# Output projection of a hybrid encoder: seven products of block halves in place of eight

## The reference, cut to what matters

```python
y_a = (on + bonus) * silu(g_a)      # RWKV heads, normalised per head, 384 columns
y_b = o * silu(g_b)                 # attention heads, 384 columns
y_c = u * sv * silu(g_c)            # spatial gating, 256 columns
y = concatenate([y_a, y_b, y_c], axis=-1) @ w_out      # (tokens, 1024) @ (1024, 1024)
return x + gate[:, None, :] * y
```

## Time and profile before

| What | us |
|---|---|
| median of 3 runs (4828.7 to 4844.89) | 4836.14 |
| profiled execution, its own time | 4841.52 |
| span of the profile | 4839.7 |
| TensorE busy in the span | 4595.1 (95%) |
| VectorE busy | 3230.5 (67%) |
| GpSimd busy | 972.8 (20%) |
| first to last matmul of L2407, layer 0 | 2115.2 to 2442.9 |
| the same, layer 1 | 4523.4 to 4834.4 |

### The profile page before, as it was taken

One profiled execution on the slowest core, in us unless ns is written; L12 is line 12 of the kernel. 1 busy time (PEld: TensorE's weight loads), 2 busy tenths in 40 slices (PEclk: granted clock), 3 DMA queues, 4 the chain that ended last, 5 costly groups with the idle time before them and its releaser, 6 DMA issues. The chain is left out here.

```text
span 4839.7 us, 121929 instructions
## 1 busy us (share of the span) xinstructions
PE 4595.1 (95%) x51708; PEld 2830.3 (58%) x51708; DVE 3230.5 (67%) x4926; ACT 1969.3 (41%) x4238; POOL 972.8 (20%) x1638
## 2 busy tenths in 40 slices
PE   7999999989997999989989999999899989999899
PEld 6788444457775445444468884444577754444454
DVE  4555378746656989966545554787466669999665
ACT  1121455535555555521111214655355655555211
POOL 3444000013332000011134440000133310000111
PEclk9999999999999999999999999999999999999999
DMA  6232556556554121155342325565566641211443
GB/s 229 95 125 88 210 175 233 181 144 165 160 160 107 30 46 33 51 176 207 126 157 96 122 76 211 186 225 182 156 164 164 170 94 29 46 40 45 166 166 115
DMA packets 577852, 647.70 MB, mean 134 GB/s; under 512 B 233936, under 2 KB 458896, under 8 KB 567712
## 3 DMA queue, kind: packets, MB, share of 16 engines
q1 hardware_dynamic: 576720, 638.81, 42.3%
q10 hardware_dynamic: 592, 1.10, 0.1%
HBM read 372.64 MB, written 267.13 MB: 132 GB/s over the span
## 5 line engine op out<-in xcount | busy, mean ns | idle before, releaser
L2083 ACT ACTIVATE att_pr<-ps,att_nb 128x512 f32<-128x512 f32 (+1 forms) x960 | 588.0, 628 | 367.1 <-DVE att_nb L2112 367.1
L2407 PE MATMUL ps<-w_out,fin_yT 128*128 128x512 f32 x1280 | 568.5, 597 | 1.3 <-ACT fin_yT L2269 1.3
L2107 DVE TENSOR_REDUCE att_mx<-ps 128x2 f32<-128x1024 f32 (+1 forms) x408 | 492.2, 1206 | 10.1 <-PE ps L2005 10.1
L2129 DVE STREAM_TRANSPOSE att_PT<-att_pr 128x1024 f32<-128x1024 f32 x384 | 473.0, 1232 | 1.0 <-ACT att_pr L2083 1.0
L2039 PE MATMUL ps<-att_PT,att_V 128*32 128x256 f32 x6144 | 408.3, 381 | 10.9 <-issue 7.7
L2407 PEld LDWEIGHTS ps<-w_out,fin_yT 128*128 128x128 f32 x1280 | 238.8, 191 | 273.4 <-issue 273.4
L2005 PE MATMUL ps<-qk 96*32 96x512 f32 (+1 forms) x3840 | 393.7, 530 | 1.5 <-ACT att_pr L2083 1.5
L625 PE MATMUL ps<-feat_Ts,feat_Ss 128*128 128x256 f32 x1680 | 374.8, 379 | 0.6 <-DVE feat_Ts L529 0.6
L1023 PE MATMUL ps<-w_both,prep_hT 128*128 128x512 f32 (+1 forms) x832 | 354.1, 581 | 0.0
L625 PEld LDWEIGHTS ps<-feat_Ts,feat_Ss 128*128 128x128 f32 x1680 | 319.5, 190 | 44.8 <-issue 1.4
L2065 POOL TENSOR_TENSOR att_mm<-att_mx,att_fold 128x8 f32<-128x8 f32 (+1 forms) x408 | 83.2, 204 | 1061.0 <-DVE att_mx L2107 1061.0
(11 more groups left out here) (300 smaller groups left out, 8673.1 us busy)
## 6 DMA issues: line engine op xcount, KB each, us to landing
s_sc<-prep_sc SPq DMA_DIRECT2D x20, 3072.0 KB, 8.9
scan_src<-s_sc SPq DMA_DIRECT2D x104, 384.0 KB, 5.1
s_qkt<-qT SPq DMA_DIRECT2D x40, 576.0 KB, 4.1
s_zf<-feat_co SPq DMA_DIRECT2D x88, 256.0 KB, 2.4
src<-s_sc SPq DMA_DIRECT2D x56, 384.0 KB, 4.9
s_ht<-feat_hT SPq DMA_DIRECT2D x10, 2048.0 KB, 17.2
s_zt<-st SPq DMA_DIRECT2D x80, 256.0 KB, 3.7
fin_z<-s_zt SPq DMA_DIRECT2D x30, 576.0 KB, 5.4
```

The lines of the kernel that those rows point to most:

```text
L2083: last = a.activation(pr[:, m % 4, w * i:w * (i + 1)], ps[:, b0 + w * i // G, w * i % G:w * i % G + w], ACT.Exp, bias=nb[:, m % 2, i:i + 1 ...
L2107: v.tensor_reduce(mx[:, m % 2, 0:n], ps[:, b0:b0 + 2, :].rearrange("p b (u k) -> p (b u) k", u=n // 2), AX.X, ALU.max).then_inc(maxed, 1)
L2129: v.transpose(into, pr[:, m % 4, :].rearrange("p (u k q) -> p u k q", u=n, q=SUB)).then_inc(flipped, 1)
L2407: last = pe.matmul(b, yT[n % TPG][:, k, :], wo[:, k, G * c:G * (c + 1)], start=(k == 0), stop=(k == KD - 1))
```

## The change: what it does

Tiles are taken in pairs p = 0 to 9. Pair 0 is multiplied as before (four `direct` halves). For pairs 1 to 9 the 256 x 1024 by 1024 x 1024 product is split into 2 x 2 blocks (A by token tile and by half of the features, B by halves of rows and columns), and seven block products P1 to P7 of 4 matmuls each replace eight:

- GpSimd makes the sums of weights once per layer (`sum_weights`, 8 instructions of 128x1024), four sums of tokens per pair (`sum_tokens`, 128x512: S1 to S4), and all four additions to the residual x (`add`, 128x512).
- ScalarE copies P1 to SBUF (`keep_first`). VectorE makes U2 = P1 + P6 and U3 = U2 + P7 (`partial`), and the blocks C11 (one instruction), C22, C21 and C12 (an addition and a multiplication by the gate each) in `block_of`.
- P1 and P2 share PSUM bank 0, P6 and P7 bank 1, P5 and P3 bank 2, P4 has bank 3. The units sv, ya, yb, yc share banks 4 and 5, by `Uses(2, BANK_U)`.
- TensorE's order for a pair is P1, P6, sv(a), P2, the turns of a, [modulation], P7, P5, sv(b), P4, the turns of b, P3, with a and b the two tiles of the next pair.
- The loads of x are taken out of the other loads of a tile and come after its store; the modulation weights have two buffers for eight; the modulation rows are turned at the stage's end.

The core of the diff (indentation shortened):

```diff
-order = []
-for n in range(NT):
-    if n == 0:
-        order += [("sv", 0), ("yc", 0), ("ya", 0), ("yb", 0)]
-    order += [("p", n, 0)]
-    if n + 1 < NT:
-        order += [("sv", n + 1), ("ya", n + 1), ("yb", n + 1), ("yc", n + 1)]
-    order += [("p", n, 1)]
-uses = Uses(BANK_M)
+PAIRS, HK = NT // 2, KD // 2
...
+BANK_X, BANK_Y, BANK_V, BANK_Z, BANK_U = 0, 1, 2, 3, 4
+DIRECT = ((0, 1), (1, 1), (0, 0), (1, 0))
+SEVEN = ("P1", "P6", "P2", "P7", "P5", "P4", "P3")
+order = [("sv", 0), ("yc", 0), ("ya", 0), ("yb", 0), ("sv", 1), ("ya", 1), ("yb", 1), ("yc", 1)]
+for n in range(2, NT):
+    order += [("sv", n), ("ya", n), ("yb", n), ("yc", n)]
+uses = Uses(2, BANK_U)
 for u in order:
     uses.add(u, "act" if u[0] in ("yb", "yc") else "dve")
...
+    B11, B12, B21, B22 = (wo[:, HK * i:HK * (i + 1), G * j:G * (j + 1)] for i in range(2) for j in range(2))
+    N1, N2, N4, N3 = wsum[:, 0], wsum[:, 1], wsum[:, 2], B12
+    S1, S2, S3, S4 = (sums[:, j] for j in range(4))
...
+            for p in range(PAIRS + 1):
+                if more and p < KD:
+                    if p >= 2:
+                        sp.wait_ge(ada_used, p - 1)
+                    sp.dma_start(ada[:, p % 2, :], d["ada_w"][:, (l + 1) * KD + p, 0:2 * D]).then_inc(ada_in[p], 16)
+                for n in (2 * p, 2 * p + 1):
+                    if n + TPG < NT:
+                        wait_turned(sp, n)
+                        load_own(n + TPG)
+                        load_heads(n + TPG)
+                if p % 2 and 2 * p + 2 < NT:
+                    wait_for(sp, ("ya", 2 * p + 1))
+                    load_gates((2 * p + 2) // TPG)
+                if p:
+                    for n in (2 * p - 1, 2 * p - 2):
+                        if p == 1:
+                            sp.wait_ge(added0, len(DIRECT))
+                        else:
+                            sp.wait_ge(added, added_at(p - 1, "C21" if n % 2 else "C12"))
+                        store(n)
+                    for n in (2 * p - 1, 2 * p - 2):
+                        if n + TPG < NT:
+                            sp.wait_ge(sent[n % TPG], 16 * here(n)[1])
+                            load_x(n + TPG)
...
+            def keep_first(p):
...
+            for n in range(NT + 2):
+                if n < NT:
+                    open_gates(n)
+                    squares(n)
+                if n % 2 == 0 and n >= 4:
+                    keep_first(n // 2 - 1)
+                if n < NT:
+                    for name in ("yb", "yc") if n else ("yc", "yb"):
+                        turned_out((name, n))
...
+            def sum_weights(n, half):
+                to, one, two = ((N1, B12, B11), (N2, B22, N1), (N4, B21, N2), (N3, B22, B12))[n]
+                k = slice(HK // 2 * half, HK // 2 * (half + 1))
+                if n in (1, 2):
+                    g.wait_ge(w_summed, 2 * n)
+                if n == 3:
+                    g.wait_ge(w_summed, 2)
+                    g.wait_ge(done, done_at(0, (1, 1)))
+                g.tensor_tensor(to[:, k, :], one[:, k, :], two[:, k, :], ALU.subtract).then_inc(w_summed, 1)
+            def sum_tokens(p, n):
+                one, two = yT[2 * p % TPG], yT[(2 * p + 1) % TPG]
+                A11, A12, A21, A22 = one[:, 0:HK, :], one[:, HK:KD, :], two[:, 0:HK, :], two[:, HK:KD, :]
+                to, a_, b_, op = ((S1, A21, A22, ALU.add), (S2, S1, A11, ALU.subtract), (S3, A11, A21, ALU.subtract), (S4, A12, S2, ALU.subtract))[n]
+                if n == 0:
+                    wait_turned(g, 2 * p)
+                    wait_turned(g, 2 * p + 1)
+                if n in (1, 3):
+                    g.wait_ge(y_summed, summed_at(p, n))
+                if p > 1:
+                    g.wait_ge(done, done_at(p - 1, ("P5", "P6", "P7", "P3")[n]))
+                g.tensor_tensor(to, a_, b_, op).then_inc(y_summed, 1)
+            def add(p, what):
+                t, j, c = {"C11": (t11, 0, 0), "C12": (t12, 0, 1), "C21": (t21, 1, 0), "C22": (t22, 1, 1)}[what]
+                n, w = 2 * p + j, slice(G * c, G * (c + 1))
+                wait_x(g, n)
+                if what == "C11":
+                    g.wait_ge(evicted, evicted_at(p, what))
+                else:
+                    g.wait_ge(gated, 3 * (p - 1) + ("C22", "C21", "C12").index(what) + 1)
+                g.tensor_tensor(x[n % TPG][:, w], x[n % TPG][:, w], t[:, :], ALU.add).then_inc(added, 1)
+            root_v(0)
+            root_a(0)
+            root_v(1)
+            sum_weights(0, 0)
+            root_a(1)
+            sum_weights(0, 1)
+            root_v(2)
+            sum_weights(1, 0)
+            sum_weights(1, 1)
+            root_a(2)
+            sum_weights(2, 0)
+            sum_weights(2, 1)
+            root_v(3)
+            sum_weights(3, 0)
+            root_a(3)
+            sum_weights(3, 1)
+            for p in range(1, PAIRS):
+                more_tiles = p + 1 < PAIRS
+                sum_tokens(p, 0)
+                sum_tokens(p, 1)
+                if more_tiles:
+                    root_v(2 * p + 2)
+                sum_tokens(p, 2)
+                if p > 1:
+                    add(p - 1, "C21")
+                    add(p - 1, "C12")
+                if more_tiles:
+                    root_a(2 * p + 2)
+                sum_tokens(p, 3)
+                add(p, "C11")
+                if more_tiles:
+                    root_v(2 * p + 3)
+                add(p, "C22")
+                if more_tiles:
+                    root_a(2 * p + 3)
+            add(PAIRS - 1, "C21")
+            add(PAIRS - 1, "C12")
...
+            def residual(i):
...
+            def partial(p, what):
+                v.wait_ge(done, done_at(p, "P6" if what == "U2" else "P7"))
+                v.wait_ge(kept, p)
+                if p > 1:
+                    v.wait_ge(evicted, evicted_at(p - 1, "C12" if what == "U2" else "C21"))
+                v.tensor_tensor((u2 if what == "U2" else u3)[:, :], s1[:, :], ps[:, BANK_Y, :], ALU.add).then_inc(evicted, 1)
+            def block_of(p, what):
+                t, bank, after = {"C11": (t11, BANK_X, "P2"), "C22": (t22, BANK_V, "P5"), "C21": (t21, BANK_Z, "P4"), "C12": (t12, BANK_V, "P3")}[what]
+                v.wait_ge(done, done_at(p, after))
+                if p > 1:
+                    v.wait_ge(added, added_at(p - 1, what))
+                else:
+                    v.wait_ge(added0, len(DIRECT))
+                if what == "C11":
+                    v.tensor_tensor(t[:, :], ps[:, bank, :], gate[:, min(p // 2, 1), 0:G], ALU.mult).then_inc(evicted, 1)
+                    return
+                v.wait_ge(evicted, evicted_at(p, "U2" if what == "C12" else "U3"))
+                v.tensor_tensor(t[:, :], (u2 if what == "C12" else u3)[:, :], ps[:, bank, :], ALU.add).then_inc(evicted, 1)
+                v.wait_ge(evicted, evicted_at(p, what))
+                v.tensor_tensor(t[:, :], t[:, :], gate[:, min(p // 2, 1), 0:G] if what == "C21" else gate[:, min(p // 2, 1), G:D], ALU.mult).then_inc(gated, 1)
+            def early(n):
+                statistics(n)
+                norm_v(n)
+                gate_b(n)
+                variance(n)
...
+            early(1)
+            gate_c(1)
+            normalise(1)
+            turn_a(1)
+            residual(0)
+            early(2)
+            residual(1)
+            gate_c(2)
+            normalise(2)
+            turn_a(2)
+            residual(2)
+            early(3)
+            gate_c(3)
+            normalise(3)
+            residual(3)
+            turn_a(3)
+            for p in range(1, PAIRS):
+                a_, b_, more_tiles = 2 * p + 2, 2 * p + 3, p + 1 < PAIRS
+                if p > 1:
+                    block_of(p - 1, "C12")
+                if more and p == PAIRS - 1:
+                    v.wait_ge(ada_used, KD)
+                if more_tiles:
+                    early(a_)
+                partial(p, "U2")
+                if more_tiles:
+                    gate_c(a_)
+                    normalise(a_)
+                block_of(p, "C11")
+                if more_tiles:
+                    turn_a(a_)
+                    statistics(b_)
+                partial(p, "U3")
+                if more_tiles:
+                    norm_v(b_)
+                    gate_b(b_)
+                    variance(b_)
+                block_of(p, "C22")
+                if more_tiles:
+                    gate_c(b_)
+                    normalise(b_)
+                block_of(p, "C21")
+                if more_tiles:
+                    turn_a(b_)
+            block_of(PAIRS - 1, "C12")
+            if more:
+                v.wait_ge(turned, 1)
+                modulation_columns(v, ps, cols[l + 1], amod, amod_s)
...
+            def unit(name, n):
+                u, j = (name, n), n % TPG
                 f = uses.former(u)
                 if f:
                     pe.wait_ge(emptied[f[0]], f[1])
-                return ps[:, uses.bank(u), :]
-
```

(88 more changed lines are left out.)

145 lines of the change are left out of this document (64 added, 81 removed).

## The result

| | before | after |
|---|---|---|
| median, us | 4840.52 (4 runs, 4828.7 to 4850.81) | 4964.56 (4 runs, 4963.81 to 4971.13) |
| profiled execution | 4841.52, span 4839.7 | 4963.81, span 4961.7 |
| the stage's products, first to last, layer 0 | 327.7 | 393.7 |
| the same, layer 1 | 311.0 | 361.5 |

The change is slower: ratio 1.026, 95% interval 1.0233 to 1.0287. The forecast was +65 us, at most +106; it is +122 by the spans and +124 by the medians. The two stages show +66.0 and +50.5. After the last product the span goes on for 6.55 us where it had 5.32, 1.23 more for GpSimd's last addition; counted twice, it brings the sum to 118.9.

The account below looks back on a forecast made before the run. TensorE, busy 95% of the span, was taken as the bound. Per layer -31.0 matmuls, +47.2 pair waits, +15.6 start, +1.4 end gave +33.2; twice, less 1.3, gave +65: 4901 us, range 4858 to 4942.

Parts of the forecast that it names:

- the four waits of a pair: TensorE ahead of sv(a), yc(a), ya(b) and yc(b): 0.94, 2.02, 1.32 and 1.74 us lost.
- matmuls saved: Nine pairs per layer save four matmuls each on TensorE: 31.0 us per layer, 62 in all.
- waits in pairs 1 to 8: TensorE waits 6.02 us a pair, less 0.94 in pair 1: 47.2 us per layer.
- waits at the start of the stage: TensorE waits around the units of tiles 1 to 3, largest 6.9 us at sv(3): 15.6 us per layer.
- GpSimd's addition at the end: After the last pair's P3 and VectorE's gating, GpSimd's addition to x adds 1.36 us per layer.
- modulation rows turned elsewhere: Layer 0: 16 small transposes leave TensorE's path, taking 1.3 us off.
- the step on TensorE's clock: TensorE in the changed stage was taken to stay at full clock, 2.4 GHz: 0 us.
- rival 2: TensorE's clock falls at the long waits, 1.7 us each, 58 us more: 4959 us; 5%.
- the walk: Step-by-step timeline of one pair on TensorE, VectorE and GpSimd: 33.57 us against 31.0, with 6.02 of waits.
- a granted clock that falls in pairs 1 to 9: Sign in TensorE's granted clock that would show the prediction wrong; no size given.
- Rival 1: VectorE's tensor_tensor does not contend with GpSimd: +29 us in all, 4866 us; 12%.
- Rival 3: Waits stay under TensorE's cover; faster if a pair's losses sum below 1.75 us, 4799 us with none; 5%.

Follow-up runs that it names:

- e3: Changed kernel with matmuls whose results nobody reads filling TensorE's four waits of a pair, both layers; 4937.3 us.
- e1: Changed kernel with sv, ya, yb, yc using four PSUM banks in turn instead of two, layer 1 only; 4920.1 us.
- e2: Changed kernel with GpSimd taking the root for the second new tile before the addition of C22 instead of behind it; 4933.4 us.
- e6: Changed kernel with GpSimd's additions to x cut from 512 to 32 columns, order and waits kept; 4894.1 us.
- f1: Changed kernel with units ordered sv, yb, yc, ya, yb straight after sv, and GpSimd's queue reordered; 4823.0 us.
- e4: Changed kernel with GpSimd's root of the first new tile before S3 and the additions C21 and C12; 4962.6 us.
- f3: f1 with the stage's start reordered: direct products parted around units, residuals after turn_a(3), sums of weights moved, own-bank waits in pair 1; 4801.8 us.
- f4: f3 with statistics of tile 4 ahead of the last two residuals, its first root ahead of two sums of weights, another sum later; 4806.5 us.
- e5: Kernel before the change with two PSUM banks for sv, ya, yb, yc and four for the product halves; 4883.3 us.

## Why the prediction was wrong

The sign was right, and the four waits of a pair came in their places. The size was not: 119 to 122 us, where 65 were forecast and 106 was the upper end. By the steps of the sum:

| step | forecast, us | measured, us |
|---|---|---|
| matmuls saved (9 x 3.45 a layer) | -62.0 | -62 (3.43 a product) |
| waits in pairs 1 to 8 | +94.4 (6.02 each) | +105.6 (6.78 each, less 1.44 in pair 1) |
| waits at the start of the stage | +31.2 | +28.3 |
| GpSimd's addition at the end | +2.7 | +2.5 (1.23 in layer 1, taken twice) |
| modulation rows turned elsewhere | -1.3 | not measured apart; -1.3 kept |
| TensorE's clock in the pairs | 0 | +35.1 |
| TensorE's clock at the start | 0 | +10.7 |
| sum | +65 | +118.9 |

- **What failed is the step on TensorE's clock**, which the sum put at 0 and which cost 46 us: some 39 in slow products, the rest in sv and transposes. Without it the same rows give +73, about 4909 and inside the range. It stood in the text as rival 2, at 5%. I priced one fall rightly (1.7 us; the pairs of layer 1 rise in steps of 1.7) and wrote "No row here shows waits of 2 us beside long products". But the walk in the same text put four waits of 1 to 2 us into every pair, and the earlier trace rows showed a clock that falls when TensorE idles and a product that pays for it. An unseen state that the forecast itself creates over 60 times deserved more than 5%, and the upper end of the range should have held more than a fall at the starts. Not every pair fell, so it stayed under rival 2's 58. The prediction's own last sign of being wrong, a granted clock that falls in pairs 1 to 9, came true: 0.90 and 0.97 over pairs 2 to 8. e3 shows the cause by itself, e1, e2 and e6 show that the clock gives time back with each wait taken away.
- **The waits in a pair** have the causes that the walk gave: e1 (banks), e2 (the root's place), e6 (GpSimd's additions) take away the ones that they should. They were undersized by 0.76 us a pair, 0.50 of it ahead of sv, since `norm_v`'s first instruction, a scalar form with one tensor from SBUF, was taken to run unhindered and took 1.36. I had the walk's hindered L2321 (L2465 now) in exchange, which ran free.
- **The start**: P1 of pair 1 starts 55.4 us (layer 0) and 53.5 us (layer 1) after `direct(0)`, forecast some 50. The waits come to 14.2 us a layer and not 15.6: sv(3) starts 6.9 us late, as worked out, but sv(2) and ya(2), with 1.2 and 0.55, start on time. The rest is the clock again: three of the four direct products take 8.6 to 10.1 us in each layer, where full clock has 7.08 and the kernel before had one such product.
- **Rival 1** (no contention for `tensor_tensor`) is refuted by L2463, L2486 and L2503 at 1.3 to 1.4 us. **Rival 3** (faster) failed by the 6.8 us of a pair, where it needed 1.75; f1 shows that its pair exists with another order. The loads of x cost nothing that the trace shows: no wait of TensorE or GpSimd in the stage is put down to them.

Left open: how much of the 39 us belongs to which wait (e2 gave 16 back for 0.95 us a pair, e6 23 for 3.2, e4 none), and why one layer falls more often than the other. Whether more can be had from the start (f3 still waits 4.8 us a layer) is open too: only f4 tried. The remaining 3.1 us between the stages' 118.9 and the spans' 122.0 weren't traced; they are small beside the 4198 to 4221 us that the rest of the program takes from profile to profile.

## What to carry to other kernels

Saved matmuls are worth only what TensorE's order lets through: with few PSUM banks in turn, put last in a tile the unit whose eviction is slowest, and put GpSimd's long SBUF instructions beside VectorE work that reads PSUM. With both, and with the start reordered, the same seven products went from 124 us slower to 38 us faster. When a forecast adds regular waits to a TensorE that was never idle, count the clock as a term of its own, not as a remote rival; filling the waits with matmuls that nobody reads is a quick test of it. And moving a contended instruction is a guess until run: two such moves (e4, f4) gained nothing.

## What the runs showed of the hardware

- TensorE's granted clock fell, in 12 of 16 pairs, between products of 3.43 us for waits of 1.2 to 2.0 us each, four in 34 us, on one core. It stayed at 1.00 in layer 1's pairs with one wait of 0.9 in each 16.6 us (e5) and with the two of 1.27 and 1.22 in 30.5 us (e1). Making TensorE do useless work in the waits kept it at 1.00 in pairs 2 to 8 and made the kernel 27 us faster.
- A `tensor_scalar` of 128x256 fp32 with its scalars from SBUF took 1.36 us beside a GpSimd addition of 128x512, 0.41 alone.
- A GpSimd sum of 128x1024 took about 2.5 us and held a VectorE instruction of 0.43 to 0.56 us for 2.44 to 2.69 us.
